# Counting the units of a routed expert stage over all experts, with one bound per expert read into registers

## The chip, the cores and the metric

The kernel runs on one core of a Trainium2 chip. The metric is device time in microseconds (us), the median of several executions. A core has five engines that run side by side and meet only at semaphores: TensorE (PE; its weight loads are listed as PEld), VectorE (DVE), ScalarE (ACT), GpSimd (POOL) and SyncE (SP, here only a queue for transfers). A name with a q behind it (PEldq, ACTq, SPq) is the sequencer of that engine: it runs the register instructions and issues transfers. All of them share 16 DMA engines.

## What is computed

One decoder layer: three mixers, then a mixture of experts, then a norm. The change lies in the expert stage. 1024 tokens each go to 2 of 64 experts; an expert is a gated MLP (1024 to 512 to 1024) in float32:

```
expert_ids = g_idx[:, None] * EXPERTS_PER_GROUP + top_loc      # 2 per token
...
def expert_block(args):
    xb, e = args
    return (jax.nn.silu(xb @ w1[e]) * (xb @ w3[e])) @ w2[e]
...
y = jnp.zeros((t, d), x.dtype).at[sorted_tok].add(y_sorted)    # weighted sum of a token's 2 results
```

Each expert has 6 MB of weights, all 64 are read, and how many tokens an expert gets is known only at run time.

## The kernel before

The tokens of an expert are cut into units of 32 (CAP); an expert has at least one unit, and this input has 100 units. The weights live in 4 places of SBUF (homes, `s`, SLOTS = 4): expert e has home e mod 4, and 16 turns `t` of 4 homes run through the 64 experts in order. Every engine runs the same nest (`each_unit`, L350 to L365): over t, over the 4 homes (unrolled), and over the units of the expert, a loop whose bounds are read from SBUF.

Three numbers per expert lie in `spans`: the first and the last unit of the expert, **counted within its home**, and the shift from that count to the count over all units. So `c` counts units within a home and `u = c + shift` counts all. Where an expert ends and the next begins, each engine's sequencer loads the three numbers (L357, L358, L359). I call that place a boundary; four boundaries make a turn.

One unit goes like this, with the names that the prediction uses:

- **gather**: POOL waits until the turning of the unit before is done (`tok_turned`), copies 32 token numbers (L653) and issues an indirect DMA that fetches their rows into xg (L657). It fetches one unit ahead.
- **turning**: PE transposes xg (L723, out dve_bank, in gain_b), once the gather has landed. DVE copies the result to xT (L1598).
- **up product**: 32 PE steps (64 records, L979) of xT with w13 of the home; then `gu_ready`. PE then turns the tokens of the next unit.
- **silu** on ACT (L1156), the product with the gate on DVE (L1603), PE turns it (L723, in gain_a), DVE copies it (L1605).
- **down product**: L993 with w2 of the home, into the home's PSUM bank; then `y_ready`.
- **copy out**: ACT copies the bank to SBUF (L1160, `y_drained`) and issues four stores to DRAM (L1163, `y_stored`). Then ACT goes on to the next unit.

The semaphores of this chain (gu_ready, silu_ready, hid_ready, hid_turned, hidT_ready, y_ready, y_drained, y_stored) exist once per home and are compared with `c`; xT_ready, tok_turned and tok_gathered exist once and are compared with `u`.

SP refills a home (`refill`, L516 to L525): for expert e it waits until the up products of expert e - 4 are done (L521), issues the table of token numbers and the two up weights (2 MB each, L467), waits for that expert's down products and issues the down weights (2 MB, L471). These transfers stand in one queue, in order. After the last refill SP loads 4 MB of rows for the end of the kernel (L534).

After the 64 experts POOL picks each token's two results, and DVE, ACT and POOL add, normalize and store them.

The numbers in `spans` come from DVE (L1567 to L1579), at the end of the routing; `routed` releases the engines into the expert stage.

Of the kernel before, what the change touches and what calls it, by code (L numbers as in the profile page):

```python
# [25 lines left out]
I32 = mybir.dt.int32  # L26
U32 = mybir.dt.uint32
ALU = mybir.AluOpType
# [23 lines left out]
E = NG * PER  # L52
# [51 lines left out]
def program(nc, x, mem, g_mix, g_mem, w_in, w_gate, b_gate, lam_re, lam_im, log_dt, b_re, b_im,  # L104
# [3 lines left out]
    with ctx:  # L108
# [44 lines left out]
        spans = sb("spans", [1, 3, SLOTS * TURNS], I32)  # L153
# [39 lines left out]
        def tiles(n, k):  # L193
# [16 lines left out]
                  for s in range(2)]  # L210
# [96 lines left out]
                    ("gu_ready", "silu_ready", "hid_ready",  # L307
                     "hid_turned", "hidT_ready", "y_ready", "y_drained", "y_stored")}
# [41 lines left out]

        def each_unit(eng, body, enter=None):


            with eng.Fori(0, TURNS) as t:
                for s in range(SLOTS):
                    at = bass.ds(t * SLOTS + s, 1)
                    first = eng.value_load(spans[0:1, 0, at], min_val=0, max_val=SLOT_UNITS)  # L357
                    end = eng.value_load(spans[0:1, 1, at], min_val=0, max_val=SLOT_UNITS)  # L358
                    shift = eng.value_load(spans[0:1, 2, at], min_val=0, max_val=UNITS)  # L359
                    if enter:  # L360
                        enter(s, t)
                    with eng.Fori(first, end) as c:
                        u = nc.s_assert_within(c + shift, 0, UNITS - 1, skip_runtime_bounds_check_because=(
                            "the units of all experts are at most UNITS"))
                        body(c, s, u, t, first)  # L365
# [5 lines left out]
        def _(sp):  # L371
# [144 lines left out]
            def refill(e, s):  # L516
                first = sp.value_load(spans[0:1, 0, bass.ds(e, 1)], min_val=0, max_val=SLOT_UNITS)
                up, down = expert(bass.ds(e, 1))

                sp.wait_ge(per_slot["gu_ready"][s], first)  # L520
# [3 lines left out]
                sp.wait_ge(per_slot["y_ready"][s], first)  # L524
# [6 lines left out]
            last = sp.value_load(spans[0:1, 1, E - SLOTS:E - SLOTS + 1], min_val=0, max_val=SLOT_UNITS)  # L531
            sp.wait_ge(per_slot["gu_ready"][0], last)
            for i in range(NT):
                sp.dma_start(h_late[:, i], h_dram[i * P:(i + 1) * P]).then_inc(h_loaded[i], 16)  # L534
            sp.wait_ge(per_slot["y_ready"][0], last)
# [11 lines left out]
        def _(pool):  # L547
# [113 lines left out]
            def unit_work(c, s, u, t, first):  # L661
                column = nc.s_assert_within(c - first, 0, COLS - 1, skip_runtime_bounds_check_because=(
# [3 lines left out]
            def expert_tokens(s, t):  # L666
# [4 lines left out]
            units = (pool.value_load(spans[0:1, 1, E - 1:E], min_val=0, max_val=SLOT_UNITS)  # L671
                     + pool.value_load(spans[0:1, 2, E - 1:E], min_val=0, max_val=UNITS))
            gather(no_token[:, :], units)
# [982 lines left out]
```

## Time and profile before

| | before |
|---|---|
| median of 3 runs | 2466.71 us (2466.71 to 2469.51) |
| profiled execution, its own time | 2457.62 us |
| its span, first to last instruction | 2455.6 us |
| mean granted PE clock | 0.872 |
| PE, PEld busy | 76%, 43% |
| DVE, ACT, POOL busy | 20%, 11%, 10% |
| bytes moved | 510.96 MB |

The expert stage runs from about 1340 us to about 2394 us of the span. In the profile a busy share is an average over stages with different limits, so the table says little about one stage; the rows below are cut by stretch. In a timeline row, the bracket gives the idle time of the engine just before the row, and what ended it. Register instructions are not counted as busy. The matmul rows of this stage have two records per instruction, and some records are missing.

### The profile page before, as it was taken

Reading aid. Unit: us, or ns where it says so; the run is one execution under the profiler, and the core shown is the slowest. Engines: PE = TensorE matmul, PEld = TensorE weight load, DVE = VectorE, ACT = ScalarE, POOL = GpSimd, SP = SyncE. Lnnn points to the kernel's source line nnn. Section 1 sums busy time; section 2 is a strip of 40 time slices with the busy share of each in tenths; the row PEclk is TensorE's granted clock in tenths of the full one; section 3 lists DMA queues with packets and bytes.
Section 4 is the critical chain, followed back from the end, with each engine's and each line's share of the span. In section 5 each row is a group of like instructions: output and inputs, shape, how many; then the busy total and the mean of one; then the engine's idle time right before and its main releaser. Section 6 shows DMA issues by size and latency. Waiting matters only on the chain.

```text
span 2455.6 us, 38793 instructions
## 1 busy us (share of the span) xinstructions
PE 1865.0 (76%) x13850; PEld 1047.8 (43%) x13851; DVE 483.4 (20%) x1173; ACT 267.0 (11%) x543; POOL 257.2 (10%) x377
## 2 busy tenths in 40 slices
PE   6455689779899999999895777778777787655550
PEld 5344545554444444444453444445444444322330
DVE  4435310330211111111355000001101111000006
ACT  3000210112000000000111000101010101000002
POOL 1490000000000000000001111111111111000004
PEclk9755699889899999999997998989989989767775
DMA  7020212000011111110636899999999997999985
GB/s 266 0 54 13 105 58 64 26 1 26 35 39 39 38 37 36 36 40 2 251 129 242 331 406 403 406 397 347 383 403 357 409 400 305 418 416 418 421 360 205
DMA packets 156775, 510.96 MB, mean 208 GB/s; under 512 B 38384, under 2 KB 88048, under 8 KB 139824
## 3 DMA queue, kind: packets, MB, share of 16 engines
q1 hardware_dynamic: 126128, 461.36, 48.5%
q0 software_dynamic: 8768, 27.02, 3.1%
q10 hardware_dynamic: 21840, 22.06, 2.6%
q8 instruction: 23, 0.38, 0.1%
q14 instruction: 16, 0.13, 0.0%
HBM read 479.71 MB, written 34.35 MB: 209 GB/s over the span
## 4 chain that ended last, share of the span: by engine, by line
PE 53%; DMA 12%; SPq 10%; DVE 8%; issue 5%; ACTq 4%; ACT 3%; POOL 3%; POOLq 0%; DVEq 0%
PE act_bank L716 23%; PE dve_bank L716 15%; DMA gain_b<-xf_rows,gather_idx 6%; SPq L521 5%; PE act_bank L979 4%; DMA unit_results<-spatialT 3%; PE act_bank L993 3%; SPq L467 3%; ACTq L1163 2%; PE dve_bank L723 2%; PE dve_bank L993 2%; SPq L471 2%; DVE unit L1227 2%; DMA tokens<-expert_token_table 1%; PE dve_bank L793 1%
## 5 line engine op out<-in xcount | busy, mean ns | idle before, releaser
L716 PE MATMUL act_bank<-norm_store,unit 128*128 128x512 f32 x896 | 394.4, 595 | 8.7 <-DVE unit L1469 8.7
L716 PEld LDWEIGHTS act_bank<-norm_store,unit 128*128 128x128 f32 x896 | 171.1, 191 | 223.7 <-issue 223.7
L979 PE MATMUL act_bank<-unit,gain_a 128*32 128x256 f32 x3520 | 211.2, 393 | 21.4 <-issue 21.0
L993 PE MATMUL act_bank<-unit,gain_a 128*32 128x256 f32 x2208 | 183.5, 488 | 39.6 <-DVE gain_a L1605 39.6
L723 PE MATMUL dve_bank<-ident,gain_b 32*128 32x32 f32 x808 | 74.4, 236 | 164.9 <-DMA gain_b<-xf_rows,gather_idx 164.6
L1603 DVE TENSOR_TENSOR gain_a<-gain_a,act_bank 128x128 f32<-128x128 f32 x100 | 28.8, 288 | 770.3 <-ACT gain_a L1156 770.3
L979 PEld LDWEIGHTS act_bank<-unit,gain_a 128*32 128x32 f32 x3520 | 125.3, 114 | 110.4 <-issue 54.2
L723 PEld LDWEIGHTS dve_bank<-ident,gain_b 32*128 32x128 f32 x808 | 64.5, 152 | 208.7 <-issue 208.7
L993 PEld LDWEIGHTS act_bank<-unit,gain_a 128*32 128x32 f32 x2208 | 92.4, 134 | 101.6 <-issue 87.6
L1481 DVE TENSOR_TENSOR rows_store<-dve_bank,rows_store 128x512 f32<-128x512 f32 x48 | 33.2, 692 | 440.8 <-PE dve_bank L716 440.8
L716 PE MATMUL dve_bank<-unit,mid_store 128*128 128x512 f32 x256 | 113.1, 601 | 8.9 <-DMA unit<-in_w_router 8.9
L716 PE MATMUL dve_bank<-unit,unit 128*128 128x512 f32 x256 | 115.1, 593 | 0.0
L716 PE MATMUL act_bank<-unit,norm_store 128*128 128x512 f32 x256 | 110.4, 593 | 0.8 <-issue 0.8
L716 PE MATMUL dve_bank<-unit 128*128 128x512 f32 (+1 forms) x320 | 104.0, 474 | 6.2 <-ACT unit L1024 6.2
L653 POOL COPY gather_idx<-tokens 32x1 int32 x100 | 17.7, 177 | 836.2 <-PE dve_bank L723 576.8
L657 POOL DMA_INDIRECT gain_b<-xf_rows,gather_idx x101 | 94.4, 935 | 83.4 <-POOL gather_idx L653 83.4
L979 PE MATMUL act_bank<-mid_store,gain_a 128*32 128x256 f32 x1536 | 91.6, 391 | 9.4 <-issue 9.3
L979 PE MATMUL act_bank<-norm_store,gain_a 128*32 128x256 f32 x1344 | 80.4, 393 | 23.5 <-issue 23.5
L993 PE MATMUL dve_bank<-rows_store,gain_a 128*32 128x256 f32 x992 | 76.3, 459 | 17.8 <-DVE gain_a L1605 17.8
L716 PEld LDWEIGHTS act_bank<-unit,norm_store 128*128 128x128 f32 x256 | 64.4, 252 | 45.7 <-issue 30.1
L1122 ACT ACTIVATE rows_store<-act_bank,gate_bias_now 128x512 f32<-128x512 f32 x48 | 33.0, 687 | 417.3 <-PE act_bank L716 417.2
L716 PEld LDWEIGHTS dve_bank<-unit,mid_store 128*128 128x128 f32 x256 | 48.8, 193 | 68.6 <-issue 68.6
(225 smaller groups left out, 1671.9 us busy)
## 6 DMA issues: line engine op xcount, KB each, us to landing
unit<-in_w SPq DMA_DIRECT2D x112, 2048.0 KB
norm_store<-in_w SPq DMA_DIRECT2D x32, 2048.0 KB
mid_store<-in_w SPq DMA_DIRECT2D x32, 2048.0 KB
rows_store<-in_w SPq DMA_DIRECT2D x16, 2048.0 KB
unit<-in_w_gate SPq DMA_DIRECT2D x24, 512.0 KB, 5.3
unit<-in_w_in SPq DMA_DIRECT2D x4, 2048.0 KB, 12.4
unit_results<-unit POOLq DMA_DIRECT2D x4, 2048.0 KB, 16.3
unit_results<-spatialT ACTq DMA_DIRECT2D x220, 32.0 KB
```

The costliest lines, as they stand in the source:

```text
L467: sp.dma_start(w13[s][:, z].rearrange("p k n -> p (k n)"), w_up[z].rearrange("e (p k) n -> p (e k n)", p=P)).then_inc(up_loaded[s], 16)
L471: sp.dma_start(w2s[s], w_down.rearrange("e (k p) n -> p (e k) n", p=P)).then_inc(down_loaded[s], 16)
L521: sp.dma_start(tokens[:, s], table_of[bass.ds(e, 1)].rearrange("e p n -> (e p) n")).then_inc(tokens_loaded[s], 16)
L657: pool.indirect_dma_start(xg, None, xf_dram, bass.IndirectOffsetOnAxis(ap=gather_idx[:, 0:1], axis=0), bounds_check=T - 1, oob_is_err=Fals ...
L716: ins = nc.tensor.matmul(out_, stationary, moving, start=first and n == 0, stop=n == len(pairs) - 1)
L723: ins = nc.tensor.transpose(bank[:, n * rows:(n + 1) * rows], block_, ident[0:rows, 0:rows])
L979: ins = nc.tensor.matmul(act_bank[0][h * CAP:(h + 1) * CAP, 0:2 * FQ].rearrange("t (w n) -> t w n", w=2), xT[:, k], w13[s][:, :, k, h * FQ ...
L993: ins = nc.tensor.matmul(y_bank[s][z * CAP:(z + 1) * CAP, 0:DQ], hidT[:, j], w2s[s][:, j, z * DQ:(z + 1) * DQ], start=j == 0, stop=j == QU ...
L1122: drained(nc.scalar.activation(gates[n % 4], act_bank[g % 4][:, :], ACT.Sigmoid, bias=gate_bias_now[:, s, i:i + 1]))
L1163: act.dma_start(y_dram[bass.ds(u * CAP, CAP), z * DQ:(z + 1) * DQ], y_rows[s][z * CAP:(z + 1) * CAP]).then_inc(per_slot["y_stored"][s], 16)
L1227: step(v.tensor_tensor(o, a, b, op))
L1481: v.tensor_tensor(parts[i], dve_bank[b % 4][:, :], gates[n % 4], ALU.mult).then_inc(dve_drained, 1)
```

## The change

One count over all units takes the place of the counts per home, except where ACT waits for its stores. `starts` holds 65 numbers: how many units lie before expert 0, 1, ..., 64. An engine reads one of them at a boundary, since the end of one expert is the start of the next; at the start of a turn it reads two. Seven of the eight semaphores of the chain exist once and are compared with `u`. `y_stored` stays per home, and so ACT keeps `spans` and its three loads. DVE writes `starts` with two more instructions.

```diff
+        starts = sb("starts", [1, E + 1], I32)
...
         per_slot = {n: [sem(f"{n}{s}") for s in range(SLOTS)] for n in
-                    ("gu_ready", "silu_ready", "hid_ready",
-                     "hid_turned", "hidT_ready", "y_ready", "y_drained", "y_stored")}
+                    ("y_stored",)}
+        gu_ready, silu_ready, hid_ready, hid_turned, hidT_ready, y_ready, y_drained = (
...
+        def start_of(eng, e):
+            return eng.value_load(starts[0:1, bass.ds(e, 1)], min_val=0, max_val=UNITS)
...
             with eng.Fori(0, TURNS) as t:
+                end = start_of(eng, t * SLOTS)
                 for s in range(SLOTS):
-                    at = bass.ds(t * SLOTS + s, 1)
-                    first = eng.value_load(spans[0:1, 0, at], min_val=0, max_val=SLOT_UNITS)
-                    end = eng.value_load(spans[0:1, 1, at], min_val=0, max_val=SLOT_UNITS)
-                    shift = eng.value_load(spans[0:1, 2, at], min_val=0, max_val=UNITS)
+                    first, end = end, start_of(eng, t * SLOTS + (s + 1))
...
             def refill(e, s):
-                first = sp.value_load(spans[0:1, 0, bass.ds(e, 1)], min_val=0, max_val=SLOT_UNITS)
+                past = start_of(sp, e - (SLOTS - 1))
-                sp.wait_ge(per_slot["gu_ready"][s], first)
+                sp.wait_ge(gu_ready, past)
...
-                pe.wait_ge(per_slot["y_drained"][s], c + 1)
+                pe.wait_ge(y_drained, u + 1)
...
-            each_unit(act, unit_work)
+            with act.Fori(0, TURNS) as t:
+                for s in range(SLOTS):
+                    at = bass.ds(t * SLOTS + s, 1)
+                    first = act.value_load(spans[0:1, 0, at], min_val=0, max_val=SLOT_UNITS)
+                    end = act.value_load(spans[0:1, 1, at], min_val=0, max_val=SLOT_UNITS)
+                    shift = act.value_load(spans[0:1, 2, at], min_val=0, max_val=UNITS)
...
+            step(v.memset(starts[:, 0:1], 0))
+            step(v.tensor_copy(starts[0:1, 1:E + 1], all_ends[0:1, :]))
             step(v.tensor_copy(spans[0:1, 0], first_unit[0:1, :]))
```

What stands on PE at a boundary (here from home 1 to home 2), before: the end of the loop over the units of one expert, nine instructions that load three numbers, and the entry of the next loop.

```order
L362 COMPARE_AND_BRANCH
L357 ISA
L357 TENSOR_LOAD spans
L357 ISA x2
L358 ISA
L358 TENSOR_LOAD spans
L358 ISA x2
L359 ISA
L359 TENSOR_LOAD spans
L359 ISA x2
L362 UNCONDITIONAL_BRANCH
L362 ISA
```

The same place on PE in the change, up to the wait in front of the up product:

```order
L366 COMPARE_AND_BRANCH
L355 ISA
L355 TENSOR_LOAD starts
L355 ISA x2
L366 UNCONDITIONAL_BRANCH
L366 ISA
L979 ISA [waits xT_ready]
```

Two of three loads are gone, and nothing else stands in between. POOL and DVE change in the same way.

On ACT at the same boundary the change still reads (the line numbers alone differ from before):

```order
L1175 COMPARE_AND_BRANCH
L1172 ISA
L1172 TENSOR_LOAD spans
L1172 ISA x2
L1173 ISA
L1173 TENSOR_LOAD spans
L1173 ISA x2
L1174 ISA
L1174 TENSOR_LOAD spans
L1174 ISA x2
L1175 UNCONDITIONAL_BRANCH
L1175 ISA
```

Nothing moved there. On DVE, at the end of the routing (lane_row holds the counts), these rows stand in the change, where before there were the last three and the scan in front of them:

```order
L1587 SCALAR_TENSOR_TENSOR lane_row<-unit_9,lane_row 128x64 [waits dve_step]
L1588 MEMSET starts 1x1 [waits dve_step]
L1589 CAST starts<-lane_row 1x64 [waits dve_step]
L1590 CAST spans<-lane_row 1x64 [waits dve_step]
L1591 CAST spans<-lane_row 1x64 [waits dve_step]
L1592 TENSOR_TENSOR spans<-lane_row 1x64 [waits dve_step]
```

Two short instructions stand ahead of `routed` that did not before.

## Rows read from the trace of the kernel before

**Rows 1.** The page, part 2: busy share of the 16 DMA engines, 40 slices.

```profile
DMA  7020212000011111110636899999999997999985
```

**Rows 2.** Stretches: length, PE, PEld, DVE, ACT, POOL busy, PE clock, DMA share, GB/s.

```profile
1660.00:1700.00 40.00, 33.63 (x513) 21.29 (x508) 3.64 (x12) 4.37 (x11) 4.76 (x9) 0.92 0.84 320
...
1880.00:1900.00 20.00, 15.46 (x251) 10.52 (x251) 2.73 (x9) 1.70 (x5) 3.33 (x6) 1.00 0.71 263
...
2020.00:2060.00 40.00, 32.10 (x521) 21.09 (x513) 4.56 (x15) 4.58 (x11) 5.56 (x10) 0.98 0.63 237
2060.00:2380.00 320.00, 190.02 (x2310) 101.42 (x2310) 20.05 (x66) 20.56 (x48) 24.45 (x44) 0.75 1.02 418
```

**Rows 3.** Waits of the SP queue, 1380 to 2060: us, times, longest.

```profile
SPq L521 <- PE act_bank L979: 405.7, 37, 34.3
```

**Rows 4.** Timeline: start, us, engine; a unit behind a boundary, then one without.

```profile
1855.51 1.93 PE L993 MATMUL act_bank<-unit,gain_a 128*32 128x256 f32 x32 [0.57 <-DVE gain_a L1605]
1855.93 0.93 POOL L657 DMA_INDIRECT gain_b<-xf_rows,gather_idx  x1 [0.82 <-POOL gather_idx L653]
...
1857.59 0.38 ACT L1160 ACTIVATE lane_row<-act_bank 128x256 f32<-128x256 f32 x1 [4.19 <-PE act_bank L993]
...
1858.78 3.66 PE L979 MATMUL act_bank<-mid_store,gain_a 128*32 128x256 f32 x64 [1.33 <-issue]
1862.50 0.28 ACT L1156 ACTIVATE gain_a<-act_bank 128x128 f32<-128x128 f32 x1 [4.53 <-PE act_bank L979]
...
1863.14 0.65 PE L723 MATMUL dve_bank<-ident,gain_b 32*128 32x32 f32 x8 [0.70 <-DMA gain_b<-xf_rows,gather_idx]
...
1864.65 1.93 PE L993 MATMUL act_bank<-unit,gain_a 128*32 128x256 f32 x32 [0.60 <-DVE gain_a L1605]
...
1865.04 0.93 POOL L657 DMA_INDIRECT gain_b<-xf_rows,gather_idx  x1 [0.82 <-POOL gather_idx L653]
...
1866.37 3.66 PE L979 MATMUL act_bank<-mid_store,gain_a 128*32 128x256 f32 x64
...
1871.25 0.65 PE L723 MATMUL dve_bank<-ident,gain_b 32*128 32x32 f32 x8 [1.21 <-DMA gain_b<-xf_rows,gather_idx]
```

**Rows 5.** PE's loads: ns min/median/max, first and last start; one boundary, then 1350:2050.

```profile
L357 PEldq SEQ_ASSERT  x1: 18/18/18, 1856.9 to 1856.9; - x1
...
L359 PEldq SEQ_ASSERT  x1: 18/18/18, 1858.4 to 1858.4; - x1
...
L358 PEldq TENSOR_LOAD <-spans x41: 297/301/325, 1352.0 to 2049.3; - x41
```

**Rows 6.** Waits in 1350 to 2050: us in total, times, longest.

```profile
POOL gather_idx L653 <- PE dve_bank L723: 555.5, 77, 12.4
...
PE dve_bank L723 <- DMA gain_b<-xf_rows,gather_idx: 56.1, 38, 16.7
...
PE dve_bank L723 <- DVE gain_a L1603: 33.9, 27, 5.4
```

**Rows 7.** The chain of waits near 1490: a boundary at which ACT came last.

```profile
1489.99 0.39 ACT lane_row L1160
...
1494.47 0.28 ACT gain_a L1156
```

**Rows 8.** Timeline: a long wait of PE, and the down product behind it.

```profile
1512.10 0.65 PE L723 MATMUL dve_bank<-ident,gain_b 32*128 32x32 f32 x8 [2.22 <-DMA gain_b<-xf_rows,gather_idx]
...
1513.72 3.64 PE L993 MATMUL act_bank<-unit,gain_a 128*32 128x256 f32 x32 [0.57 <-DVE gain_a L1605]
```

**Rows 9.** Waits in 2100 to 2380.

```profile
POOL gather_idx L653 <- DMA tokens<-expert_token_table: 235.1, 17, 14.1
```

**Rows 10.** Timeline: a cast of the routing, then the first unit.

```profile
1338.14 0.25 DVE L1577 CAST spans<-lane_row 1x64 int32<-1x64 f32 x1
...
1353.86 6.19 PE L979 MATMUL act_bank<-norm_store,gain_a 128*32 128x256 f32 x64 [2.08 <-issue]
...
1359.98 0.68 PE L723 MATMUL dve_bank<-ident,gain_b 32*128 32x32 f32 x8
```

More of the change, by code:

```diff
@@ L306, in program @@
         per_slot = {n: [sem(f"{n}{s}") for s in range(SLOTS)] for n in
-                    ("gu_ready", "silu_ready", "hid_ready",
-                     "hid_turned", "hidT_ready", "y_ready", "y_drained", "y_stored")}
+                    ("y_stored",)}
+        gu_ready, silu_ready, hid_ready, hid_turned, hidT_ready, y_ready, y_drained = (
+            sem(n) for n in ("gu_ready", "silu_ready", "hid_ready", "hid_turned", "hidT_ready", "y_ready", "y_drained"))
         picked = [sem(f"picked{b}") for b in range(PICKS)]
@@ L523, in refill @@
                 expert_up(up, s)
-                sp.wait_ge(per_slot["y_ready"][s], first)
+                sp.wait_ge(y_ready, past)
                 expert_down(down, s)
@@ L670, in _ @@
             each_unit(pool, unit_work, expert_tokens)
-            units = (pool.value_load(spans[0:1, 1, E - 1:E], min_val=0, max_val=SLOT_UNITS)
-                     + pool.value_load(spans[0:1, 2, E - 1:E], min_val=0, max_val=UNITS))
-            gather(no_token[:, :], units)
-            last = [pool.value_load(spans[0:1, 1, e:e + 1], min_val=0, max_val=SLOT_UNITS) for e in last_of]
+            gather(no_token[:, :], start_of(pool, E))
+            last = [pool.value_load(spans[0:1, 1, e:e + 1], min_val=0, max_val=SLOT_UNITS)
+                    for e in range(E - SLOTS, E)]
             for s in range(SLOTS):
@@ L970, in turn_tokens, with work @@
                 turn(dve_bank[0], [xg[:, k * P:(k + 1) * P] for k in range(KD)], CAP).then_inc(tok_turned, 1)
-            def work(c, s, u, t, first):
+            def work(u, s, t, first):
                 pe.wait_ge(xT_ready, u + 1)
@@ L1148, in _, with unit_work @@
             act.wait_ge(weighted, 1)
+            act.sem_inc(y_drained, 1)
             for s in range(SLOTS):
[L1151 removed]
                 act.sem_inc(per_slot["y_stored"][s], 16 * QUARTERS)
[L1154 to L1157 removed]
+            def unit_work(c, s, u):
+                act.wait_ge(gu_ready, u + 1)
+                nc.scalar.activation(silu_g, act_bank[0][:, 0:FQ], ACT.Silu).then_inc(silu_ready, 1)
+                act.wait_ge(y_ready, u + 1)
                 act.wait_ge(per_slot["y_stored"][s], c * (16 * QUARTERS) + 16 * QUARTERS)
[L1160 to L1161 removed]
+                nc.scalar.activation(y_rows[s], y_bank[s][:, 0:DQ], ACT.Copy).then_inc(y_drained, 1)
+                act.wait_ge(y_drained, u + 2)
                 for z in range(QUARTERS):
@@ L1164, in unit_work @@
                                   y_rows[s][z * CAP:(z + 1) * CAP]).then_inc(per_slot["y_stored"][s], 16)
-            each_unit(act, unit_work)
+            with act.Fori(0, TURNS) as t:
[4 more added lines that the diff above has]
+                    shift = act.value_load(spans[0:1, 2, at], min_val=0, max_val=UNITS)
+                    with act.Fori(first, end) as c:
+                        unit_work(c, s, nc.s_assert_within(c + shift, 0, UNITS - 1, skip_runtime_bounds_check_because=(
+                            "the units of all experts are at most UNITS")))
             def scale(i):
```

43 lines of the change are left out of this document (18 added, 25 removed).

## The prediction, made before the kernel was run

> **What bounds the kernel now.** I began with the line of the DMA engines' share. It jumps to 9 when the expert stage starts and stays there to its end, but for one 7 [rows 1]. The stage reads 64 x 6 MB of weights, so the first candidate is the weight stream. Cut into stretches, the share says more: 1.02 is what a full stream reads here, over 320 us from 2060 on. It is clearly below in three places: 0.84 over 40 us, 0.71 over 20 us, 0.63 over 40 us [rows 2]. The missing part is (1.02 - 0.84)/1.02 x 40 = 7.1, then 6.1 and 15.3, together 28.5 us in which the stream stood still.
>
> Why it stood still is in the waits of the SP queue: it waited 37 times for PE's up product before it could refill a home [rows 3]. So there are two halves. Up to about 2046 us (the end of the last pause) the end of the stage is set by how fast PE gets through units, since that ends the pauses. After it every expert has one unit, POOL waits for token tables that stand behind weights in the queue (235 us in 17 waits [rows 9]), and only bytes count. **A microsecond saved on the units before 2046 shortens a pause and moves the end by one; a microsecond saved later moves nothing; and the total is capped by 28.5 us.**
>
> So the question is what paces a unit before 2046. The timeline shows three chains that meet at each unit [rows 4].
> - PE: from the start of a turning to the down product 1.51 us (1863.14 to 1864.65), down product and up product 5.38 (1864.65 to 1866.37 + 3.66), together 6.9 within an expert. Behind a boundary it is 1.51 + (1858.78 + 3.66 - 1855.51 = 6.93) = 8.4.
> - The gather: turning, POOL's copy, issue, landing, next turning. From 1863.14 to 1871.25 that is 8.1: 1.9 to the issue and 6.2 from there. The gather before took 7.2 from its issue (1855.93 to 1863.14), a cycle of 9.1.
> - ACT: copy out, four stores, the loads, silu.
> A turning waited for the gather 38 times out of 77 [rows 6]: the gather paces about half of the units, PE or ACT the others.
>
> **The change part by part.**
>
> *PE's loads.* A load is closed by a check of its value. From the check behind the first of the three loads to that behind the third it is 1858.4 - 1856.9 = 1.5 us, so 0.75 per load with its register instructions; the load alone is 0.30 [rows 5]. Two go, 1.50 us. Before, PE's gap in front of the up product is 1.33 at a boundary, and within an expert the up product even overlaps the down product by 0.2 (1866.37 against 1864.65 + 1.93) [rows 4]. Hence the one load that stays hides under the down product, and the boundary costs PE nothing any more: 8.4 becomes 6.9. There are 41 such places before 2050 [rows 5], the entry into the first turn among them; every fourth, 11 of them, stands at the start of a turn and loses one (0.75), 30 lose two. If all of it counted, 30 x 1.50 + 11 x 0.75 = 53 us, more than the cap. It can't all count, because 6.9 is less than the gather's 8.1 to 9.1. What a boundary saves is what the gather leaves: nothing where the turning waited already (in rows 4 PE was ready at 1862.44 and waited 0.70; it will wait 2.2), up to 1.5 where the gather had landed long before.
>
> The Trainium skill ("DMA: Bandwidth & Descriptors", section "Latency and other measured facts") gives a floor of about 600 ns for such a load. This trace shows 0.75 us with the register instructions and 0.30 without, so the page lies between. By the page two loads would save 1.2 us in place of 1.5, and the sum below would shrink by a fifth.
>
> *Walking through the units.* I took the 76 units before 2046 in order, kept each gather's time from issue to landing, each store and each product, moved PE's up products forward by 1.50 or 0.75, and let each turning, silu and product start at the last of its releasers. In 23 of the 30 two-load boundaries the turning did not wait for the gather, but in most of these the gather lands within half a microsecond. About ten keep a saving, 0.4 to 1.5 each, 8.4 in all, and it is not lost in the units after.
>
> *The first unit.* Its up product started at 1353.86 after 2.08 us of loads [rows 10]; one load less, 0.75. The turning behind it, at 1359.98, didn't wait for its gather, so this one counts in full, and the first refill starts as much earlier. Sum so far 9.1.
>
> *ACT.* It keeps its three loads, and it is close behind PE: silu follows the copy out by 4.91 in rows 4, where PE released it, and by 4.48 where ACT itself came last [rows 7]. So the silu path gains at most 0.43 per boundary, then ACT is late. The walk has this in it. It costs little, since the turning goes ahead of it on PE and the gather starts from the turning.
>
> *What the removed gap did.* The gap and the wait for the gather stood apart, 1.33 and 0.70 us, and the down product behind them took 1.93 [rows 4]. Where PE waited 2.22 us at one go, the down product took 3.64 [rows 8], 1.71 more: the granted clock was 1.2 GHz in place of 2.4. With the gap gone, nine or ten boundaries get one wait of 1.8 to 3.2 us, while about six present long waits get shorter. Most of a slow down product hides under the gather (6.9 + 1.7 = 8.6 against 8.1 to 9.1). I take 1.5 of them as uncovered, 1.5 x 1.71 = 2.6.
>
> *POOL and DVE.* Their two loads per boundary run while POOL waits for the turning (555.5/77 = 7.2 us each [rows 6]) and DVE for silu. Nothing.
>
> *Waits over all units.* SP's condition is the same one: expert e - 4 is through. The one wait that becomes wider is PE's for `y_drained`: the down product now needs the copy of the unit before, whatever its home. ACT does copy and silu in order, and this product needs the silu of its own unit, so the condition is always met. Nothing; and were it not, it would be 0.38, the copy.
>
> *DVE's two instructions.* About 0.25 each, as the cast next to them [rows 10], 0.5 before `routed`. POOL goes through one load less there and then waits for the token table, so the first gather doesn't move; the last weights of expert 3 start 0.5 later and are needed only at the fourth expert. Nothing, at most 0.5 lost.
>
> **Sum**: 9.1 - 2.6 = 6.5 us. Against the profiled execution, 2457.6 becomes 2451.1. That execution was 9 us faster than the median of the timed runs; a difference passes to them as it is, 2466.7 - 6.5 = **2460.2 us**.
>
> **The rivals.**
>
> *A, the gather and the clock take nearly all* (gain 0 to 4.9, taken 2.5: 2464). If the gather slows with a denser stream, or if all ten slow down products fall on PE-paced units, the saved gap turns into waiting. For it: 38 of 77 turnings wait already. Against it: the first unit's 0.75 and several boundaries with 1 us of room.
>
> *B, slower through the clock.* One mechanism: every two-load boundary now ends in one long wait of PE, the following down product runs at 1.2 GHz, and ACT, which copies out after it and keeps its loads, then releases silu at 1.51 + 3.64 + 0.15 + 4.48 = 9.8 after the turning [rows 4, 7, 8], where the next turning comes at 9.1; PE waits again, and the next product is slow too. One such pair costs 1.7 to 3.4 us on a path without cover. From six of them on, 9.1 is used up; with ten, 17 us, the kernel is 8 slower: 2475. For it: 33.9 us of waits for silu stand in the trace, up to 5.4 [rows 6]. Against it: a unit that was slow has cover from the gather in most places.
> The Trainium skill ("TensorE: Matmul & The Clock Gate", section "HAM oscillation") tells of a kernel whose clock falls at every wait for a transfer between short bursts of products. Rows 8 agree for one wait of 2.22; rows 4 show that two shorter ones don't do it. By the page, B is what happens.
>
> *C, more of the room is real* (gain 12 to 28: 2447). If stores and gathers land sooner when units are spaced evenly, the pauses close. The cap of 28.5 bounds it.
>
> *D, the change doesn't do what it says*: registers are short, and `end` is read again or copied at cost. The listing shows one load per boundary. Chance 0.02, time as before.
>
> **How the numbers follow.** Forecast (gain 4.9 to 12) 0.50; A 0.31; C 0.06; B 0.11, of which 0.03 stay within 0.2%; D 0.02. A time within 0.2%, 4.9 us, is about what can't be told from no change here. Faster 0.50 + 0.06 = 0.56; within 0.2% 0.31 + 0.03 + 0.02 = 0.36; slower 0.08. The range reaches from a gain of 14.2 (2452.5) to a loss of 1.3 (2468.0); outside are most of B and C and a little of the rest, together under 0.2.
>
> **What would show it.** Right: PE's gap at two-load boundaries at 0, or overlapped; about 41 + 11 loads of PE before 2050; the last pause of the stream ending 5 to 12 us earlier against the start of the stage; the three shares below 1.02 rising; the waits for token tables after 2100 as before, 14 us each (235.1/17); the waits of the turning for the gather longer by 20 us or more in total. Wrong: a PE clock clearly under 0.92 in 1660 to 1700 [rows 2] and its neighbours; more waits for silu than 27; a gap that stays. If the last pause ends at the same time, A holds.

## The result and the profile after

| | before | after |
|---|---|---|
| median of 20 runs | 2468.14 us | 2475.65 us |
| mean granted PE clock of a run | 0.864 to 0.874, mean 0.869 | 0.851 to 0.857, mean 0.854 |
| span of the profiled execution | 2455.6 us | 2476.4 us |

The change takes 1.0029 times as long, interval 1.0021 to 1.0037: 7.5 us lost where 6.5 were forecast as a gain. One of the 20 runs of before took 3032 us, as did one of `before_act_early` below (at a clock of 0.627); all ratios and intervals leave such runs out. The result goes in the direction of rival B, which had a chance of 0.11. The two profiled executions lie 20.8 us apart, because that of before (2457.6 us) is faster than any of the other timed runs. Where a sum needs a partner at a typical time, I take a run of the experiments (`pe_three_b`, 2467.78 us).

The windows of after (columns as in [rows 2], which they answer), and behind them the whole stretch up to the last pause of the weight stream:

```profile
1660.00:1700.00 40.00, 34.02 (x489) 21.68 (x493) 4.26 (x14) 3.03 (x9) 5.58 (x10) 0.87 0.85 327
1880.00:1900.00 20.00, 16.17 (x234) 9.47 (x230) 1.82 (x6) 1.32 (x4) 2.60 (x5) 0.84 0.99 375
2020.00:2060.00 40.00, 33.90 (x500) 20.81 (x493) 3.65 (x12) 3.17 (x10) 4.46 (x8) 0.89 0.85 327
2060.00:2380.00 320.00, 191.71 (x2420) 112.25 (x2419) 21.24 (x70) 23.06 (x53) 25.65 (x46) 0.76 0.99 407
...
1350.00:2067.00 717.00, 564.36 (x7951) 348.94 (x7952) 68.76 (x226) 67.75 (x165) 84.77 (x152) 0.86 0.94 367
```

The same stretch of before, up to the same unit:

```profile
1350.00:2046.00 696.00, 532.67 (x7953) 325.02 (x7953) 68.76 (x226) 67.69 (x165) 84.46 (x152) 0.92 0.96 378
```

The clock (third number from the end) reads 0.87, 0.84 and 0.89 where it was 0.92, 1.00 and 0.98, and 0.86 over the stretch where it was 0.92. The three DMA shares rose, one of the prediction's signs of being right, but the pauses lie elsewhere now: over the whole stretch the share fell from 0.96 to 0.94. The unit whose turning stood at 2045.66 us before now turns at 2066.74, and the last pause ends there instead.

The boundary did what the change says. PE's loads at the one line that is left, and SP's wait of [rows 3], here in 1380 to 2067:

```profile
L355 PEldq TENSOR_LOAD <-starts x50: 297/308/502, 1351.9 to 2028.3; - x50
...
SPq L525 <- PE act_bank L982: 439.8, 38, 36.4
```

There are 50 loads where there were three times 41. SP waited 34 us longer for PE than before, so the stream stood longer. PE's waits in 1350 to 2067 (us in total, times, longest; compare [rows 6]):

```profile
PE dve_bank L726 <- DMA gain_b<-xf_rows,gather_idx: 67.2, 40, 16.9
PE dve_bank L726 <- DVE gain_a L1616: 45.6, 36, 7.0
...
PE act_bank L982 <- issue: 6.0, 7, 1.0
```

The gap in front of the up product is 6.0 us in all. The waits for the gate product, that is for silu, went from 27 to 36 times and from 33.9 to 45.6 us. The waits for the gather grew by 11 us, where 20 or more were expected. ACT shows why silu comes late. Its waits in the same stretch:

```profile
ACT gain_a L1159 <- PE act_bank L982: 144.0, 39, 12.6
...
ACT gain_a L1159 <- issue: 91.1, 23, 5.0
```

and before, with PE's gap behind them (1350 to 2050):

```profile
ACT gain_a L1156 <- PE act_bank L979: 209.1, 54, 13.0
...
PE act_bank L979 <- issue: 43.4, 33, 2.1
...
ACT gain_a L1156 <- issue: 28.0, 8, 4.3
```

A silu preceded by "issue" waited for nothing but ACT's own sequencer. So before, PE's up product released silu 54 times and ACT came late 8 times. Now ACT comes late in 23 cases, with stores and loads in front of silu. (14 more units of each kernel have a load of ACT's function table in front of silu and stand in neither row; see the last experiments.)

The chain of waits of after, 1411 to 1443 us (start, us, what), shows where that leads. It is one loop, run three times:

```profile
1413.49 0.28 ACT gain_a L1159
...
1415.05 3.29 PE act_bank L996 x32
1418.45 0.39 ACT lane_row L1163
...
1421.00 0.29 ACTq L1172
...
1421.62 0.28 ACTq L1173
...
1422.23 0.28 ACTq L1174
...
1422.92 0.29 ACT gain_a L1159
...
1424.48 3.60 PE act_bank L996 x32
1428.19 0.39 ACT lane_row L1163
1428.74 0.33 ACTq L1166
...
1432.68 0.29 ACT gain_a L1159
...
1434.24 3.13 PE act_bank L996 x32
...
1442.05 0.29 ACT gain_a L1159
```

The steps are a slow down product (3.1 to 3.6 us instead of 1.93), ACT's copy out, four stores (L1166), three loads (L1172 to L1174), silu, gate product, PE's turning of it, and the next slow down product. The three loads start 0.62 and 0.61 us apart, which is what one costs ACT. The rounds, from silu to silu, take 9.4, 9.8 and 9.4 us; rival B worked out 9.8. The gather isn't in the loop.

### The profile page after: what moved, and what is told of

Its sections match the earlier page's. It is cut to its first block, busy times and chain, and to the rows that moved or that the text cites. A ratio compares the mean times of both kernels' runs of the same rounds, so it can differ in the third digit from the quotient of the medians.

```text
span 2476.4 us, 37345 instructions
## 1 busy us (share of the span) xinstructions
PE 1895.1 (77%) x13850; PEld 1079.8 (44%) x13851; DVE 483.4 (20%) x1175; ACT 267.3 (11%) x543; POOL 257.6 (10%) x377
## 4 chain that ended last, share of the span: by engine, by line
PE 55%; DMA 18%; DVE 8%; issue 5%; ACTq 5%; ACT 3%; POOL 3%; SPq 2%; POOLq 0%; DVEq 0%
PE act_bank L719 22%; PE dve_bank L719 15%; DMA gain_b<-xf_rows,gather_idx 8%; DMA tokens<-expert_token_table 7%; PE act_bank L996 5%; PE act_bank L982 3%; ACTq L1166 3%; DMA unit_results<-spatialT 3%; PE dve_bank L726 2%; PE dve_bank L996 2%; DVE unit L1238 2%; PE dve_bank L796 1%; SPq L525 1%; PE dve_bank L872 1%; POOL gain_a L580 1%
## 5 line engine op out<-in xcount | busy, mean ns | idle before, releaser
L996 PE MATMUL act_bank<-unit,gain_a 128*32 128x256 f32 x2208 | 203.3, 531 | 39.9 <-DVE gain_a L1618 37.0
L982 PE MATMUL act_bank<-unit,gain_a 128*32 128x256 f32 x3520 | 218.3, 401 | 0.0
L982 PEld LDWEIGHTS act_bank<-unit,gain_a 128*32 128x32 f32 x3520 | 138.7, 119 | 78.9 <-issue 27.3
L996 PEld LDWEIGHTS act_bank<-unit,gain_a 128*32 128x32 f32 x2208 | 99.9, 144 | 110.2 <-issue 99.6
L996 PE MATMUL dve_bank<-rows_store,gain_a 128*32 128x256 f32 x992 | 86.6, 508 | 17.9 <-DVE gain_a L1618 17.9
L726 PE MATMUL dve_bank<-ident,gain_a 128*128 128x128 f32 x100 | 37.1, 371 | 57.0 <-DVE gain_a L1616 52.7
```

What stands on the lines that cost most here:

```text
L726: ins = nc.tensor.transpose(bank[:, n * rows:(n + 1) * rows], block_, ident[0:rows, 0:rows])
L982: ins = nc.tensor.matmul(act_bank[0][h * CAP:(h + 1) * CAP, 0:2 * FQ].rearrange("t (w n) -> t w n", w=2), xT[:, k], w13[s][:, :, k, h * FQ ...
L996: ins = nc.tensor.matmul(y_bank[s][z * CAP:(z + 1) * CAP, 0:DQ], hidT[:, j], w2s[s][:, j, z * DQ:(z + 1) * DQ], start=j == 0, stop=j == QU ...
```

## The experiments

Every run was compared with the kernel before on the same chip. The counts of slow down products, and those of the table below, cover the first 76 units of the stage in each profiled execution. A down product is called slow when it takes more than 2.9 us, from its first record to its last. In before it takes 1.93 us where the granted clock was 1.00 (at 1855.51) and 3.64 where it was 0.50 (at 1513.72). Some recorded expectations name 33 slow products for after and 15 for `filler4`. Those counts are low: counted whole, they are 40 and 18. The likely reason is that a product that crosses the edge of a printed stretch of the timeline is shown too short there.

### Is it PE's gap?

`pe_three` puts two unused loads per boundary back, on PE alone; `pool_dve_three` does so on POOL and DVE alone:

```diff
                     first, end = end, start_of(eng, t * SLOTS + (s + 1))
+                    if eng in padded:
+                        for _ in range(2):
+                            start_of(eng, t * SLOTS + (s + 1))
```

> The changed kernel, with two more register loads at every boundary on PE alone (their values are not used); POOL, DVE, SP, ACT, the waits and the two DVE instructions of the routing stay as changed. Theory T (rival B of the prediction: with the gap gone, PE's waits merge, the down product behind them runs at 1.2 GHz, ACT is late with the next silu): the gap of about 1.3 us in front of the up product is back and splits the wait, so the time returns to that of before, 2464 to 2470 us (7 us less than the 2475.7 of the change), the mean clock from 0.854 to about 0.87, and slow waits for silu fall from 36 to below 30 before 2060 us. Rival R1 (it comes from something else: the later start, the earlier POOL and DVE, the one wait over all units): the time stays at 2472 to 2479 and the clock at 0.854. My walk in the prediction (gap removal is a gain of 9): 2480 or more.

Measured: 2475.37 us, 1.0031 (1.002 to 1.0041); mean clock 0.8645 over its runs. The time spoke for R1, the clock in part for T. In the trace, PE now did four loads at the start of a turn, and its gaps there were 2.3 us (1.75 before). So the run was not the undoing that I had meant.

> The changed kernel, with two more register loads at every boundary on POOL and on DVE (values not used), PE with one. Theory T: these loads lie under waits, so nothing changes: 2472 to 2479 us, clock 0.85 to 0.86. Rival R1 in the form that POOL or DVE, two loads lighter, disturb the order of the gathers: back to 2464 to 2470, clock about 0.87. If the loads cost something here: over 2480.

Measured: 2477.8 us, 1.0046 (1.0032 to 1.006), clock 0.854. The intervals of this run and of the change overlap: POOL's and DVE's loads don't matter, as the prediction said.

`count_only` gives all three engines their three loads back, and leaves the waits over all units, SP's refills and DVE's two instructions as changed:

> The changed kernel with its waits counted over all units, its two DVE instructions and SP's refills as they are, but PE, POOL and DVE load three numbers at each boundary again, as before. So it is the change without the loads taken out. After the run with two more loads on PE alone, which kept 2475.4 us, two theories are left. R1a (the loss is in what that run kept: the waits over all units, or the two DVE instructions with the later start): 2472 to 2479. R1b (it needs the lighter POOL or DVE together with PE, or four loads at the start of a turn, which the PE-only run had and before has not): back to 2464 to 2470.

Measured: 2469.22 us, 1.0004 (0.9995 to 1.0013), clock 0.869. The loss is gone, so it lies in the removed loads.

`before_dve2` adds to the kernel before just this:

```diff
+            step(v.memset(starts[:, 0:1], 0))
+            step(v.tensor_copy(starts[0:1, 1:E + 1], all_ends[0:1, :]))
```

> The kernel before with the change's two DVE instructions at the end of the routing (a memset and a cast into 65 numbers that nothing reads). R1d (the later start of the stage, measured as 1 us in the profiled run of the change, sets off a loss of its own): 2470 to 2476. R1c (the waits over all units are the loss): 2467 to 2469, at most the 0.25 to 1 us of the start more than before. The prediction said 0 to 0.5.

Measured: 2468.46 us, 1.0 (0.9991 to 1.0009). The two instructions cost nothing that shows.

`pe_three_b` repairs the first run:

```diff
+                        for _ in range(2 if s else 1):
+                            start_of(eng, t * SLOTS + (s + 1))
```

> The changed kernel with PE alone loading three numbers at every boundary, as before: two more loads at three of four boundaries, one more at the start of a turn (the earlier run had two more there too, four loads and a gap of 2.3 us, before 1.75). POOL, DVE, SP, ACT and the waits as changed. Theory T (PE's gap alone is what matters, and the fourth load explains why the earlier run stayed slow: eleven such places, 0.55 us each, 6 us): 2466 to 2471 us, mean clock 0.868 to 0.870, slow down products 25 or fewer of 76. Rival R1b' (POOL or DVE must be heavier too): 2473 to 2478, clock 0.865 or less.

Measured: 2467.78 us, 0.9995 (0.9986 to 1.0003); clock 0.863 to 0.875, mean 0.868; 25 slow down products, the most that T allowed. Two register loads on PE at a boundary, whose values nobody uses, take the whole loss away. Its waits in 1350 to 2058 us, and its window:

```profile
PE dve_bank L731 <- DMA gain_b<-xf_rows,gather_idx: 66.0, 45, 17.0
PE act_bank L987 <- issue: 34.9, 28, 2.0
...
PE dve_bank L731 <- DVE gain_a L1622: 27.4, 20, 4.8
...
1350.00:2058.00 708.00, 542.75 (x7947) 328.65 (x7947) 68.71 (x226) 67.49 (x164) 84.45 (x152) 0.90 0.95 372
```

Against after this is a balance of PE's time, at two spans 8.3 us apart. The change takes 34.9 - 6.0 = 28.9 us of gaps. It gives back 564.36 - 542.75 = 21.6 in longer products (the same 7950 records) and 45.6 - 27.4 = 18.2 in waits for silu. The wait for the gather grows by 1.2. That makes 12.1 us more, and the two windows differ by 9.0; smaller rows, not shown, hold the rest.

### Is it ACT's loads?

`act_early` is the changed kernel with ACT's loads moved into the unit, where ACT waits for the down product:

```diff
                 nc.scalar.activation(silu_g, act_bank[0][:, 0:FQ], ACT.Silu).then_inc(silu_ready, 1)
+                ahead = numbers(t * SLOTS + (s + 1)) if s < SLOTS - 1 else None
                 act.wait_ge(y_ready, u + 1)
```

> The changed kernel, in which ACT loads the three numbers of the next expert between its silu and the wait for the down product, in every unit, in place of at the boundary (three of four boundaries; at the start of a turn they stay). Theory T: the second half of the loop (down product slow, copy out late, three loads, silu late) loses its 1.8 us of loads, silu follows the copy out by 2.9 to 3.2 us instead of 4.5 to 4.9, waits for silu before 2060 fall from 36 to below 25, the clock rises to 0.87 or more and the time falls by 8 to 20 us, to 2456 to 2467. If only the merged wait counts and ACT does not (rival R2: the slow down product itself is the loss): the time stays within 3 us of 2475 and the clock at 0.855. If the loads in between now delay the copy out: over 2478.

Measured: 2465.83 us, 0.9991 (0.9981 to 1.0002), 10 us less than the change. The clock stayed at 0.8565 and 32 down products were slow. Its rows in 1350 to 2053 us:

```profile
PE dve_bank L726 <- DMA gain_b<-xf_rows,gather_idx: 74.0, 44, 17.1
PE dve_bank L726 <- DVE gain_a L1620: 35.1, 21, 5.9
...
ACT gain_a L1159 <- issue: 18.4, 8, 2.4
```

ACT is late 8 times in place of 23. Slow products stay, but they cost little once ACT doesn't pass them on. This was T in time and not in the clock.

> The kernel before with ACT's loads for the next expert placed between its silu and its wait for the down product (three of four boundaries), all else as before. In the changed kernel this edit gave 10 us. T (the change made ACT the late one; before it, PE's own loads hid ACT's): here it gives 0 to 4 us, 2463 to 2468, and the mean clock does not fall. R5 (ACT's loads cost the same 10 us in both kernels, so the edit says nothing about the change): 2455 to 2460.

Measured: 2466.35 us, 0.9998 (0.9988 to 1.0009). The edit that gave 10 us in the changed kernel gives nothing clear in the kernel before. The likely reason, not tested apart, is that PE's own loads run beside ACT's there. This pair also holds a first answer on the change itself: with ACT's loads early, the kernel with it (0.9991) and the one without it (0.9998) can't be told apart, although 32 down products are slow in the one and 19 in the other.

`before_act_five` adds two unused loads on ACT alone, to the kernel before:

> The kernel before with two more loads on ACT at every boundary (values not used), five in place of three, 1.2 us; PE's gap stays. If the loss is a matter of the balance between PE and ACT (PE 1.1 us earlier or ACT 1.2 us later is the same): 2474 to 2482. If the gap's splitting of the wait protects the clock: less than half of it, 2468 to 2472, clock 0.866 or more.

Measured: 2491.76 us, 1.0096 (1.0082 to 1.0111), far beyond both theories. At 0.6 us a load (the chain of after) they add about 41 x 1.2 = 49 us to ACT before the last pause, and half of that, 23 us, came out at the end. ACT had little slack in the kernel before. Waits in 1350 to 2077 us:

```profile
PE dve_bank L728 <- DVE gain_a L1609: 59.7, 32, 5.7
...
ACT gain_a L1161 <- issue: 75.7, 16, 5.5
```

The waits for silu are above even those of the change, with PE's gap in place.

### Is it the clock?

`filler4` keeps PE busy in front of each wait for the gather; `filler2` is the same with two products:

```diff
                 ins.then_inc(gu_ready, 1)
+                for _ in range(4):
+                    nc.tensor.matmul(dve_bank[3][:, 0:P], ident[:, :], ident[:, :], start=True, stop=True)
                 turn_tokens(u + 1)
```

> The changed kernel, in which PE does four more products of a 128 by 128 identity with itself, into a bank that nothing reads, between each up product and the wait for the gather (about 0.33 us each at full clock from the row of the same shape, 1.3 us in all). Theory T (PE's long idle wait lowers the clock): single waits shrink by up to 1.3 us, fewer down products take 3.6 us, clock 0.87 to 0.89; in places without a wait for the gather the four products cost up to 1.3 us each, so the time lies between 2458 and 2476. Rival R3 (the slow down products have nothing to do with how long PE is idle): the clock stays at 0.855 or lower and the time rises by 10 us or more, to 2485 and up.

Measured: 2477.36 us, 1.0047 (1.0031 to 1.0063), clock 0.875, 18 slow down products: the clock of T, but a time between the ranges of both theories. The clock was above that of before, and the kernel wasn't faster than the change: the four products took 1.16 us in every unit.

> The changed kernel with two of the unread products (0.58 us) between each up product and the wait for the gather, in place of four. Four gave clock 0.875 and 2477 us: slow down products fell from 33 to 15 and the waits for silu from 48 to 20 us, but 1.16 us stood in every unit, so gain and cost cancelled. Clock theory: half the cost, most of the effect: clock 0.862 to 0.870, 2466 to 2474. Order theory: the cost alone, without gain: 2475 to 2482.

Measured: 2478.59 us, 1.0032 (1.0016 to 1.0047), clock 0.862, 35 slow: the clock of the first theory and the time of the second. The runs spread from 2467 to 2488 us. Half the filler kept little of the effect.

> The run with ACT's loads early (2465.8 us, clock 0.8565), and two unread products (0.58 us) before each wait for the gather. If slow products still cost time once ACT's loads are out of the way: below 2464, faster than both kernels. If they no longer do (the cover of the gather takes them): 2466 to 2472, the products' own cost, though the clock rises to 0.865 or more.

Measured: 2470.49 us, 1.0011 (0.9999 to 1.0023), clock 0.865: 4.7 us slower than `act_early` by the medians, with a higher clock (the intervals just touch). With ACT out of the way the higher clock bought nothing that paid for the two products.

`gap_fill` has the delay of `pe_three_b`, but PE works in it (four unread products of 1.16 us together, at three of four boundaries):

> As the run that put PE's loads back (gap about 1.12 us, 2467.8 us, clock 0.866 to 0.869), but at three of four boundaries PE does four 128 by 128 products into an unread bank (1.16 us, read from the filler run) in place of the two loads; at the start of a turn the one extra load stays. Same delay, PE busy in it. Order theory (only when PE arrives matters): 2466 to 2470, like that run. Clock theory with idle time of any kind counting: the clock rises to 0.872 or more, slow down products under 16 of 76, and 2460 to 2466. If filling makes one unbroken busy stretch followed by one whole wait, as in the changed kernel, and it is the wait's being whole that counts: clock 0.855 to 0.865 and 2470 to 2477.

Measured: 2474.35 us, 1.0022 (1.0012 to 1.0032), clock 0.867 to 0.873. No theory fits: the order theory wanted 2468, the clock theory less, and the third a low clock. Its twelve runs lie in two groups, three at 2467 to 2468 and nine from 2472 to 2477, and the profiled one, with 21 slow products, is of the first. The nine have clocks of 0.867 to 0.872, about that of before, so a low mean clock isn't what makes them longer. Why they are stays open.

| | time | clock | slow down products of 76 | ... of these, next unit waits for silu | after the others |
|---|---|---|---|---|---|
| before | 2468 | 0.869 | 19 | 7 of 19 | 11 of 57 |
| pe_three_b | 2468 | 0.868 | 25 | 7 of 25 | 8 of 51 |
| after | 2476 | 0.854 | 40 | 21 of 40 | 8 of 36 |
| act_early | 2466 | 0.857 | 32 | 11 of 32 | 7 of 44 |
| before_act_five | 2492 | 0.863 | 28 | 14 of 28 | 18 of 48 |

A wait for silu counts in this table when PE's turning of the gate product waited more than 0.5 us. In after, all 20 down products with a PE wait of 1.5 us or more between the up product and them were slow, 9 of 12 with a longest wait of 1.0 to 1.5 us, and 11 of 44 with less; before, 13 of 17, 1 of 5 and 5 of 54. So both halves of rival B's mechanism are in the trace: a long wait goes with a slow product, and a slow product goes with a wait for silu in the unit behind it, most clearly in the changed kernel. These are counts of one execution each. The last row shows that ACT alone, made later, costs far more time with 12 slow products fewer than after.

### ACT lighter in other ways

`act_one` gives ACT one load too and counts the stores over all units, so that the copy out waits for all stores of the unit before:

> The changed kernel with ACT treated as the others: one load at a boundary, and the stores counted over all units, so that the copy out of a unit waits for the stores of the unit before it, whatever its home. T with ACT's loads as the limit: silu 1.2 us nearer to the copy out, 6 to 12 us less than the change, 2464 to 2470. Against it: a store takes 8 to 10 us to land in the chain of waits, and within an expert the copy out waits for it already; if that now holds at every boundary, copies come later and the time is 2480 or more.

Measured: 2499.59 us, 1.0127 (1.0112 to 1.0143). The warning came true, and T, whose range ended at 2470, did not. Store waits of ACT's copy in the window up to the same unit are 38, in after 11:

```profile
ACT spatialT L1162 <- DMA unit_results<-spatialT: 98.9, 13, 9.4
ACT lane_row L1162 <- DMA unit_results<-lane_row: 72.8, 11, 9.8
```

`store_one` issues one store of 128 KB per unit in place of four of 32 KB:

```diff
-                for z in range(QUARTERS):
-                    act.dma_start(y_dram[bass.ds(u * CAP, CAP), z * DQ:(z + 1) * DQ],
-                                  y_rows[s][z * CAP:(z + 1) * CAP]).then_inc(per_slot["y_stored"][s], 16)
+                act.dma_start(y_dram[bass.ds(u * CAP, CAP)].rearrange("t (z n) -> z t n", z=QUARTERS),
+                              y_rows[s]).then_inc(per_slot["y_stored"][s], 16)
```

> The changed kernel with one store per unit in place of four (the same 32 rows of 4 KB, one transfer with a three-dimensional address). ACT issues for 0.45 us in place of 1.8. Theory T (ACT's path from copy out to silu is what turns slow down products into a loss): silu 1.3 us nearer to the copy out in every unit, so at least the gain of the earlier loads, 2455 to 2466, though the clock may stay near 0.855. If ACT's path were no limit: 2473 to 2478. If a store as one transfer lands later (copies out wait for stores 11 times, 76 us in the changed kernel): over 2478.

Measured: 2599.43 us, 1.0539 (1.0517 to 1.0561). This is the third branch: ACT issued for less time, and the data landed far later. In the chain of waits of `store_one` one store takes

```profile
1456.12 26.94 DMA unit_results<-spatialT
...
1483.63 17.83 DMA unit_results<-spatialT
```

and in that of the kernel before, where four go out:

```profile
1449.89 8.38 DMA unit_results<-spatialT
```

> The changed kernel with both ACT edits: one store per unit, and the next expert's loads between silu and the wait for the down product. T: ACT is out of the way; what is left is the gather, 2450 to 2462, under both kernels. If the two edits take the same time twice: as the better of the two alone.

> The kernel before with the same two ACT edits; the only difference to the run ahead of it is the change itself. If the change is worth something once ACT is out of the way (what the prediction's walk said, 5 to 9 us): this one is 3 to 10 us slower than the run ahead, 2457 to 2466. If the gather's cycle takes what PE saves whatever ACT does (rival A of the prediction): within 2 us of it.

Measured: 2594.12 us, 1.0503 (1.0485 to 1.052), and 2613.0 us, 1.0581 (1.0567 to 1.0594). Long waits for stores stand in both, so they don't answer the question about the gather. Of the pairs with and without the change this is the only one in which the kernel with the change is clearly faster, by 19 us. Why is not known.

`table_once_early` and `before_table_early` put it again. To the early loads they add one column of silu ahead of the stage:

```diff
             act.wait_ge(weighted, 1)
+            step(nc.scalar.activation(silu_g[:, 0:1], consts[:, 0:1], ACT.Silu))
```

In every kernel above, ACT loads its function table again in front of the silu of the units of home 0 (14 times in the stretch), as in this row of after:

```profile
1558.52 1.28 ACT L1159 ACT_TABLE_LOAD   x1 [4.49 <-issue]
...
1559.82 0.28 ACT L1159 ACTIVATE gain_a<-act_bank 128x128 f32<-128x128 f32 x1
```

With the extra column these loads are gone from the loop. The Trainium skill ("ScalarE: Activation LUTs", section "What ACT_TABLE_LOAD costs") gives 1283 ns for the load, which the row agrees with, and 1380 ns more for a drain; the silu starts 0.02 us behind the load, so no drain shows.

> The changed kernel with two things taken from ACT's path: the next expert's numbers are loaded between silu and the wait for the down product (as in the run that gave 2465.8 us), and one silu of one column stands ahead of the expert stage, so that the function table is not loaded again in front of the silu of every unit of home 0 (14 loads of 1.28 us in the stage of the changed kernel). Theory T (ACT is the engine that decides): another 5 to 14 us, 2452 to 2461. If the early loads already take ACT out of the way: 2464 to 2467. If the gather and the weight stream take what ACT saves: within 3 us of 2466 as well, with more waits for the gather.

> The kernel before with the same two ACT edits; what differs from the run ahead is the change alone. If the change pays once ACT is out of the way (the walk of the prediction, 5 to 9 us): 3 to 10 us slower than that run. If PE's saved time becomes waits for the gather and slow down products whatever ACT does: within 2 us of it.

Measured: 2463.91 us, 0.9981 (0.9972 to 0.999), clock 0.857; and 2461.39 us, 0.9966 (0.9953 to 0.9979), clock 0.871. Theory T's 2452 to 2461 did not come; the second run, forecast within 2 us or 3 to 10 us slower, is 2.5 us faster. Both beat the kernel before; the better one doesn't have the change. The intervals overlap, so the change is worth nothing, or a little less, when ACT is out of the way. What became of PE's saved time shows in `table_once_early`, 1350 to 2050 us:

```profile
PE dve_bank L726 <- DMA gain_b<-xf_rows,gather_idx: 84.6, 47, 16.7
PE dve_bank L726 <- DVE gain_a L1621: 19.6, 10, 4.0
```

and in `before_table_early`, 1350 to 2051 us:

```profile
PE dve_bank L723 <- DMA gain_b<-xf_rows,gather_idx: 71.5, 45, 16.6
PE dve_bank L723 <- DVE gain_a L1616: 23.4, 11, 3.7
```

The saved gaps (40.4 us in `before_table_early`, 5.0 in `table_once_early`) become 13 us more of waits for the gather and 22 us more of down products, 202 in place of 180, with 35 slow ones in place of 20.

## Why the prediction was wrong

Step by step:

- **Only PE's progress before the last pause counts.** Right. The turning that ends the last pause comes 8.7 us later in after than in `pe_three_b` (2066.74 against 2058.01), and the spans differ by 8.3. The waits for token tables behind it kept their size, 242.4 us in 18 (235.1 in 17 [rows 9]).
- **The removed loads free PE at a boundary.** Right: gaps of 43 us became 6.
- **"The first unit ... 0.75".** The time from the first turning to the first up product did shrink, from 3.11 us (1350.75 to 1353.86) to 2.17 (1351.71 to 1353.88). In the profiled execution the stage began 0.96 later, so it doesn't show at the up product; the first turnings of all the runs lie from 1350.3 to 1353.8, so one execution can't tell how much of that is the change.
- **POOL, DVE, the waits over all units, DVE's two instructions.** Right, at nothing: 2477.8 with POOL's and DVE's loads back, 2469.22 with the counts alone, 2468.46 with the two instructions alone.
- **"Slow products: I take 1.5 of them as uncovered, 2.6 us".** This term was mis-sized. The number of waits of 1.8 us and more rose as forecast, from 13 to 17, and all 17 products behind them were slow. But behind shorter waits, which the prediction left out, 23 of 59 products were slow, before 7 of 63. In all there were 40 slow products, against 19 before and 25 in `pe_three_b`, and PE's products took 21.6 us longer than in `pe_three_b`.
- **"ACT keeps its loads ... it costs little, since the turning goes ahead of it on PE".** This is the step that failed. The turning does go ahead, but the down product waits for silu, ACT's copy out waits for the down product, and the next silu stands behind the copy: a loop through ACT that the gather isn't part of. Its slack was small before (1.2 us more per boundary on ACT, 49 in all, cost 23). Moving ACT's loads to where ACT waits gave 10 us in the changed kernel and nothing clear before: without this term the loss of 7.5 us is gone. My walk kept every product's duration, so it could not see the slow down product enter this loop. It allowed ACT to be late, and not to be made later.
- **The walk's 9.1 us.** Not there. With ACT's loads early and four stores in both kernels the change gained nothing, and nothing again with the table load gone too. In the second pair the saved gaps went into the gather and into longer down products.

Rival B had the loop, its 9.8 us, its sign and nearly its size (8 us lost against 7.5). Its condition, six such pairs, I held to be unlikely with "a unit that was slow has cover from the gather in most places". Of 40 slow products, 21 were followed by a wait for silu all the same. What in the profile spoke for B, the 33.9 us of waits for silu, weighed more than I let it: they meant that silu already ended PE's waits 27 times in 76 units. Rival A came nearest to what happened in the two pairs with ACT's loads early.

The Trainium skill ("TensorE: Matmul & The Clock Gate", section "HAM oscillation") describes a kernel whose clock falls at every wait of 3 to 5 us between bursts of products. The prediction took from this that "By the page, B is what happens". That went too far, since B's waits are of 1.8 to 3.2 us. The trace of the changed kernel agrees with the Trainium skill in kind: products behind waits of 1.5 us and more ran slow, and the clock over the stretch went from 0.92 to 0.86. The Trainium skill counts the time at the low clock as a loss. By that alone a higher clock should give the time back, and here that doesn't hold: `filler4` had 0.875 and 2477 us, `act_early` 0.857 and 2466.

What stays open: how much of the 7.5 us the clock carries. Bringing the gap back and moving ACT's loads each take the loss away, so it needs both. That the slow products are the link between them is not shown: it rests on the counts of the traces, and `gap_fill`, made to test it, fitted no theory.

## What to carry to other kernels

PE and ACT did the same small work, three loads, side by side. Where two engines of one loop do that, taking it from one of them can move the limit to the other. Before removing a small cost in such a loop, find the engine that keeps it, and add a little to that engine alone. If the kernel gets longer by a large part of what you added (here by 23 of 49 us), don't count on the saving on the other engine. Where a wait at a boundary is in front of products, sum what the products will take at the lower clock and not only the waits.

## What the runs showed of the hardware

- What a register load costs the kernel depends on the engine that does it. Two more per boundary on ACT cost the kernel before 23 us (`before_act_five`). Two on POOL and DVE cost the changed kernel nothing that shows (`pool_dve_three`), and two on PE (one at the start of a turn) made it 8 us faster (`pe_three_b`). The load itself took 0.30 us on PE.
- Beside the weight stream, the last of four stores of 32 KB landed in 8.4 us in the chain of before, and one store of the same 128 KB in 18 and 27 us in that of `store_one`.
- The function table of ACT was loaded again in the units of one home and in none of the others, 14 times 1.28 us in this stretch. No load stood in front of the copies or of the silus of the other homes. One column of silu ahead of the loop stopped it (`table_once_early`, `before_table_early`: none in the stretch).
- Four 128 by 128 products in front of each wait for the gather raised PE's mean clock from 0.854 to 0.875, over the 0.869 of before, without a gain in time (`filler4`, 2477 us).
- Down products behind a single wait of PE of 1.5 us or more took over 2.9 us in place of 1.93 in 20 of 20 cases in after and in 13 of 17 before.
